# Sparse attention's keys and queries laid out by half heads: an elementwise rotary step and logits of two 64-row products

## The chip, the cores and the metric

The program runs on one core of one Trainium2 chip. The metric is the device time of one execution in microseconds (us), the median of several. Before the change it is 1267.69 us (three runs, 1267.61 to 1268.04).

## The reference, cut to what matters

One first block (16 meta tokens and 256 tokens of width 1024, a gated delta rule branch, a sparse attention branch, an MLP) is followed by a second block. The change touches the sparse attention branch alone. Its queries have 8 heads of 128, its keys 2 heads of 128 (query head h goes with key head h // 4), and both are rotated by position:

```python
def _apply_rope(x, cos, sin):
    half = x.shape[-1] // 2
    xf = x.astype(jnp.float32)
    x1, x2 = xf[..., :half], xf[..., half:]
    ...
    return jnp.concatenate([x1 * c - x2 * s, x2 * c + x1 * s], axis=-1).astype(x.dtype)

def _dsa_branch(q, k, v, qi, ki, wi, rope_att, rope_idx, n_visible):
    q = _apply_rope(q.reshape(B_, T_, ATT_HEADS, ATT_HD), cos_a, sin_a)
    k = _apply_rope(k.reshape(B_, T_, ATT_KV_HEADS, ATT_HD), cos_a, sin_a)
    qi = _apply_rope(qi.reshape(B_, T_, IDX_HEADS, IDX_HD), cos_i, sin_i)
    ki = _apply_rope(ki.reshape(B_, T_, 1, IDX_HD), cos_i, sin_i)[:, :, 0]
    ...
        s = jnp.einsum('bqhd,bsd->bqhs', qib, ki)
        s = jnp.einsum('bqhs,bqh->bqs', jax.nn.relu(s), wib).astype(jnp.float32)
        ...
        _, idx = lax.top_k(s, topk)
        ...
        logits = jnp.einsum('bqgrd,bqkgd->bqgrk', qg, k_sel).astype(jnp.float32) * (ATT_HD ** -0.5)
```

## The kernel before, in words

**Weights.** All projections read one stream of 1 MB slots (`stream`, 256 output columns each). SyncE fetches slot s + 4 into the ring of four when TensorE has finished slot s (`slot_done`). ScalarE rounds a slot to fp32r (`whi`, line 506), VectorE, or for six slots GpSimd, makes the rest (`wlo`, lines 513 and 831), and TensorE adds three products for every tile (line 540, `mm3`), 48 matmuls for a slot. So nearly all of TensorE's time is line 540 and, for the layers that end on tokens, line 702.

**The attention part.** TensorE, ScalarE and VectorE all walk the list `PROJECT`, each doing its part of a step. The slots are `iq` (2), `av`, `ak`, `aq` (4), then `gb`, `z` and `ga` (4 each, the gates). A projection lands in one of two double banks of PSUM, and ScalarE copies it out (`project_out`, lines 1059 to 1070) and frees the pair (`pair_free`). A `rot` step is the rotary step of one tile or two: TensorE multiplies them by a signed permutation (`rotation`, line 2391, constant `turna` or `turni`) into one of the four small PSUM banks (`aux`), and VectorE makes ctmp = turned x sin (line 1655), x = x cos (line 1658), x = x + ctmp (line 1659) in `rotate`. Steps 0 to 2 are the index key and the index queries, 3 and 4 the two key heads, 5 to 8 the query heads two by two. The query rotations lag: the queries of slot j are turned after slot j + 1, the last ones after two eighths of gate slot 0.

**Selection.** `("idx", t, half)` makes four index heads' scores for query block t: TensorE (line 2400) multiplies 64-row operands, even heads in partitions 0 to 63, odd ones in 64 to 127. ScalarE takes relu, VectorE sums them (lines 1672 and 1675). `("top", t)` finds the 64 largest of each row on VectorE in eight rounds (lines 1688 and 1689), and leaves a bias (lines 1690 and 1692). The width is 144 for t = 0 and 272 for t = 1.

**Logits.** When `rope` stands at 9 (all nine rotations are done), TensorE makes one 128-row matmul a head (line 2431) into an `aux` bank; VectorE scales it and adds the bias (line 1762), takes the maximum (line 1766); ScalarE takes exponentials. The logits stand between pieces of gate slots: `gate_part(n, k0, k1)` does the eighths k0 to k1 of slot n, six matmuls each.

```python
            gate_part(0, 0, 2)
            rotation(8)
            gate_part(0, 2, 5)
            pe.wait_ge(S("rope"), 9)
            logits(0, 0, 4)
            ...
            for q in range(4):
                logits(1, 2 * q, 2 * q + 2)
                gate_part(1, q, q + 1)
```

GpSimd makes the rest of gate slot 0 once `rope` is 6, of slots 1 and 2 once it is 9.

Of the kernel before, what the change touches and what calls it, by code (L numbers as in the profile page):

```python
# [21 lines left out]
ALU = mybir.AluOpType  # L22
# [3 lines left out]
P = 128  # L26
D = 1024
KT = D // P
NCOL = 256
META = 16  # L30
QLO = META - 4
SEQ = 256
# [32 lines left out]
for _name, _count in PARAMS:  # L65
# [5 lines left out]
CONST1 = [("ident", 128), ("window", 32), ("upper", 128), ("upper16", 128), ("ones16", 128), ("spread", 128), ("head", 8),  # L71
          ("levels", 4 * 128), ("cosa", T1), ("sina", T1), ("cosi", T1), ("sini", T1), ("turna", 128),
          ("turni", 128), ("past", 2 * T1)]
# [8 lines left out]
for _name, _count in CONST2:  # L82
# [7 lines left out]
PROJECT = [("rot", 0), ("iq", 0), ("iq", 1), ("rot", 1), ("rot", 2), ("av", 0), ("idx", 0, 0), ("lo", "aq", 1), ("l2", 0),  # L90
           ("l2t", 0), ("sel", 0), ("idx", 0, 1), ("ak", 0), ("avt", 0), ("top", 0), ("cum", 0), ("idx", 1, 0), ("lo", "aq", 2), ("rot", 3), ("rot", 4),
           ("aq", 0), ("idx", 1, 1), ("lo", "aq", 3), ("aq", 1), ("rot", 5), ("top", 1), ("aq", 2), ("rot", 6), ("aq", 3),
           ("rot", 7)]

# [47 lines left out]
def program(nc, stream, params, const1, const2, x_in, x_tok, gains, y_out):  # L142
    ctx = ExitStack()
    with ctx:
# [249 lines left out]

        ROT = ["rot_ik", "rot_iq0", "rot_iq1", "rot_ak0", "rot_ak1"] + [f"rot_aq{n}" for n in range(4)]
        for step in PROJECT:
# [6 lines left out]
            elif step[0] in ("l2", "l2t", "sel", "cum"):  # L403
                use_next({"l2": "l2sum"}.get(step[0], step[0]))
        use_next(ROT[8])
        for t in range(2):
            use_next(*[f"log{t}_{hh}" for hh in range(H1)])
        for t in range(2):
# [430 lines left out]
        def pool_body(pool, own):  # L839

            pool.wait_ge(S("rope"), 6)
            pool_low(pool, FIRST["gb"], FIRST["gb"] + 1)
            pool.wait_ge(S("rope"), 9)
            pool_low(pool, FIRST["gb"] + 1, FIRST["gb"] + 3)
            pool.wait_ge(S("prob"), 4)
            pool_low(pool, FIRST["z"], FIRST["z"] + 3)

            pool.wait_ge(S("nglo"), 4)
            pool.dma_start(c2[:], const2).then_inc(c2_in, 16)
            pool.dma_start(ht[:], x_tok).then_inc(S("ht_in"), 16)  # L850
            pool.wait_ge(S("merged"), 4)
            pool_gain(pool, "wout")
            pool.wait_ge(S("h_postmix"), 9)
            pool_gain(pool, "down")

            pool.wait_ge(S("rqk"), 1)
            pool_gain(pool, "ro")
            for k in range(2):
                def tail(s0, it, j):

                    n0 = k * FT2 + j
                    pool.wait_ge(S("f_silu"), n0 + 1 + 4 * it)
                    if n0 >= 2:
                        pool.wait_ge(S("f_hi"), n0 - 1 + 4 * it)
                    nc.gpsimd.tensor_tensor(fu[:, s0 % 2], fs[:, s0 % 2], ft[:, s0 % 2, 1], ALU.mult)\  # L865
                        .then_inc(S("f_prod"), 1)
                    pool.wait_ge(S("f_prod"), n0 + 1 + 4 * it)
                    pool.wait_ge(S("f_hi"), n0 + 1 + 4 * it)
                    nc.gpsimd.tensor_tensor(flo[:, bass.ds(j + 4 * it, 1)], fu[:, s0 % 2].unsqueeze(1),
                                            fhi[:, bass.ds(j + 4 * it, 1)].bitcast(F32), ALU.subtract).then_inc(S("f_lo"), 1)  # L870
                slots(pool, f"fu{k}", tail)
                pool.wait_ge(S(["h_postret", "h_postdiff"][k]), 9)
                pool_gain(pool, f"fd{k}")
                if k == 0:
                    pool.wait_ge(S("dn_root"), 1)
                    pool_gain(pool, "do")
# [744 lines left out]
        def dve_body(dve, own):  # L1621
# [29 lines left out]
            def rotate(step):  # L1651
# [8 lines left out]
                dve.wait_ge(S("rope"), step + 1)  # L1660

            def scores(t, half):

# [75 lines left out]
            for step in PROJECT:  # L1739
                if step[0] == "iq":  # L1740
                    load_lo(FIRST["iq"] + step[1] + 3, 0)
                elif step[0] == "rot":
                    rotate(step[1])
                    if step[1] == 2:
                        decay_finish()
                elif step[0] == "idx":
                    scores(step[1], step[2])
# [6 lines left out]
                elif step[0] == "lo":  # L1754
                    low_of(step[1], step[2])
            rotate(8)
            for t in range(2):
                W = META + P + t * P
                lm = lms[t]
                for hh in range(H1):  # L1760
# [3 lines left out]
                for hh in range(4, 8):  # L1764
                    after(dve, f"log{t}_{hh}")
# [329 lines left out]
        def rotations():  # L2095
            yield "rot_ik", ik[:].unsqueeze(1), T1, "cosi", "sini", 0
            for n in range(2):
                yield f"rot_iq{n}", iq[:, 2 * n:2 * n + 2], SEQ, "cosi", "sini", META
            for n in range(2):
                yield f"rot_ak{n}", ak[:, n:n + 1], T1, "cosa", "sina", 0  # L2100
            for n in range(4):
                yield f"rot_aq{n}", aq[:, 2 * n:2 * n + 2], SEQ, "cosa", "sina", META

# [222 lines left out]
        def pe_body(pe):  # L2326
# [51 lines left out]
            def rotation(step):  # L2378
                name, x, W, c, sn, t0 = todo[step]
                turn = cst("turni" if c == "cosi" else "turna")  # L2380
                if name == "rot_ik":
                    pair_done(pe, 0)
                elif name[:6] == "rot_iq":
                    pair_done(pe, pair_first["iq"] + int(name[6:]))
                elif name[:6] == "rot_ak":
                    pair_done(pe, pair_first["ak"])
                else:
                    pair_done(pe, pair_first["aq"] + int(name[6:]))
                b = fill(name)
# [37 lines left out]
            def logits(t, h0, h1):  # L2427
                W = META + P + t * P
                for hh in range(h0, h1):
                    b = fill(f"log{t}_{hh}")  # L2430
                    is_full(nc.tensor.matmul(b[:, 0:W], aq[:, hh, t * P:t * P + P], ak[:, hh // 4, 0:W], start=True,
                                             stop=True), f"log{t}_{hh}")

            for step in PROJECT:
# [14 lines left out]
                elif step[0] in STEP_SLOTS:  # L2449
                    project(step[0], step[1])  # L2450
            gate_part(0, 0, 2)
            rotation(8)
            gate_part(0, 2, 5)
            pe.wait_ge(S("rope"), 9)
            logits(0, 0, 4)
# [545 lines left out]
def constants():  # L3001
# [14 lines left out]
    for tag, dim in (("a", 128), ("i", 64)):  # L3016
        inv = (f(10000.0) ** (-np.arange(0, dim, 2, dtype=f) / f(dim))).astype(f)
        ang = pos[None, :] * inv[i % (dim // 2)][:, None]
        c["cos" + tag], c["sin" + tag] = np.cos(ang), np.sin(ang)
        turn = np.zeros((P, P), f)  # L3020
        for m in range(P):
            lo = m % dim < dim // 2
            turn[m + dim // 2 if lo else m - dim // 2, m] = -1.0 if lo else 1.0
        c["turn" + tag] = turn
    past = [np.where(pos[None, :] <= (META + t * P + i)[:, None], 0.0, -BIG) for t in range(2)]
# [13 lines left out]
def laid_out(v):  # L3039
    w = v["w_in"][0]  # L3040
    at = np.cumsum([0, 1024, 1024, 1024, 1024, 8, 8, 1024, 256, 256, 512, 64, 8, 1024, 1024])
    gq, gk, gv, gz, gb, ga, aq, ak, av, iq, ik, iw, gate_a, gate_b = (w[:, a:b] for a, b in zip(at[:-1], at[1:]))
    small = np.concatenate([ik, ik, gb, ga, iw, np.zeros((D, NCOL - 152), w.dtype)], 1)
    ain = v["a_w_in_2"][0]
    kv = v["w_kv_2"]
# [55 lines left out]
```

## Time and profile before

| what | value |
|---|---|
| median of three runs | 1267.69 us (1267.61, 1267.69, 1268.04) |
| span of the profiled execution, first to last instruction | 1268.2 us |
| TensorE matmuls | 9041, busy 1254.3 us (99%) |
| TensorE weight loads | busy 1169.6 us (92%) |
| VectorE | busy 919.6 us (73%) |
| ScalarE | busy 699.2 us (55%) |
| GpSimd | busy 154.3 us (12%) |
| DMA queue of the weights | 46.9% of 16 engines' span |
| mean granted clock of TensorE | 0.998 of full speed |

The span stands 0.5 us above the median; no time of its own but the span is recorded for the profiled execution. In the profile PE is TensorE's matmuls, PEld its weight loads, DVE VectorE, ACT ScalarE, POOL GpSimd. Matmuls overlap in the array, so the durations of single ones add up to more than the time they take; what one costs is read from start to start. A matmul of plain fp32 operands has two records and two weight loads for each instruction, one of fp32r operands has one. The attention part lies between 90 and 210 us of the span.

### The profile page before, as it was taken

How to read it: one execution, taken by the hardware profiler on the slowest of the kernel's cores; microseconds unless marked ns; L12 is line 12 of the kernel's file. 1: busy time of each engine (PE TensorE's matmuls, PEld its weight loads, DVE VectorE, ACT ScalarE, POOL GpSimd, SP SyncE). 2: the span in 40 equal slices, each digit the busy share in tenths (PEclk: the TensorE clock that was granted, in tenths of full speed). 3: DMA queues.
4: the chain of work that ended last, by engine and by line, in shares of the span. 5: the costliest groups of instructions: out<-in, count | busy, mean ns of one | idle time of the engine just before them, and what ended most of it. 6: DMA issues, size and time to landing. Idle time of an engine off the chain costs nothing.

```text
span 1268.2 us, 23324 instructions
## 1 busy us (share of the span) xinstructions
PE 1254.3 (99%) x9041; PEld 1169.6 (92%) x9041; DVE 919.6 (73%) x1290; ACT 699.2 (55%) x1082; POOL 154.3 (12%) x113
## 2 busy tenths in 40 slices
PE   9999999999999999999999999999999999999998
PEld 8997999999989998889998989999889998999986
DVE  6886874878778774447734547999758777999954
ACT  5556465654456343345354546666547567766642
POOL 0000142000000000000000001642200000464310
PEclk9999999999999999999999999999999999999999
DMA  7552332322355555555553444555564444454562
GB/s 300 189 173 101 133 134 101 133 68 68 152 197 188 195 179 185 198 170 182 183 209 109 156 173 167 198 169 195 194 221 171 162 154 163 167 188 175 197 224 93
DMA packets 30315, 212.83 MB, mean 168 GB/s; under 512 B 3488, under 2 KB 3616, under 8 KB 5152
## 3 DMA queue, kind: packets, MB, share of 16 engines
q1 hardware_dynamic: 29088, 206.53, 46.9%
q0 software_dynamic: 1152, 5.24, 1.1%
q8 instruction: 55, 0.90, 0.3%
q14 instruction: 20, 0.16, 0.0%
HBM read 210.71 MB, written 1.05 MB: 167 GB/s over the span
## 4 chain that ended last, share of the span: by engine, by line
PE 86%; DVE 8%; ACT 4%; DMA 1%; issue 1%; SPq 0%; DVEq 0%; ACTq 0%
PE lin L540 50%; PE lin L702 21%; DVE wlo L513 3%; PE lin L2883 2%; PE lin L567 2%; ACT whi L506 2%; PE lin L569 1%; DMA raw<-in_stream 1%; PE aux L2627 1%; PE aux L2599 1%; PE aux L2485 1%; ACT lm L1377 1%; PE aux L725 1%; PE aux L2745 1%; PE aux L2555 1%
## 5 line engine op out<-in xcount | busy, mean ns | idle before, releaser
L513 DVE TENSOR_TENSOR wlo<-raw,whi 128x2048 fp32r<-128x2048 f32 x183 | 427.4, 2338 | 170.8 <-ACT whi L506 170.1
L506 ACT CAST whi<-raw 128x2048 fp32r<-128x2048 f32 x192 | 365.3, 1906 | 179.5 <-DMA raw<-in_stream 147.0
L540 PE MATMUL lin<-xhi,whi 128*128 128x256 f32 (+2 forms) x1616 | 461.5, 286 | 1.0 <-DVE wlo L513 1.0
L540 PE MATMUL lin<-xlo,whi 128*128 128x256 f32 (+2 forms) x1616 | 457.0, 283 | 0.0
L540 PE MATMUL lin<-xhi,wlo 128*128 128x256 f32 (+2 forms) x1616 | 454.7, 281 | 0.0
L540 PEld LDWEIGHTS lin<-xhi,whi 128*128 128x128 f32 x1616 | 304.1, 188 | 3.0 <-DVE wlo L513 1.2
L540 PEld LDWEIGHTS lin<-xhi,wlo 128*128 128x128 f32 x1616 | 306.1, 189 | 0.0
L540 PEld LDWEIGHTS lin<-xlo,whi 128*128 128x128 f32 x1616 | 304.6, 189 | 0.4
L865 POOL TENSOR_TENSOR fu<-fs,ft 128x256 f32<-128x256 f32 x44 | 86.2, 1958 | 259.4 <-ACT fs L1479 259.4
L2292 DVE SCALAR_TENSOR_TENSOR ft<-fy,par,ft 128x254 f32<-128x254 f32 (+1 forms) x176 | 109.5, 661 | 5.9 <-DVE ft L2292 0.2
L540 PE MATMUL lin<-whi,xhi 128*128 128x256 f32 x256 | 74.2, 290 | 0.0
L540 PE MATMUL lin<-wlo,xhi 128*128 128x256 f32 x256 | 71.9, 281 | 0.0
L540 PE MATMUL lin<-whi,xlo 128*128 128x256 f32 x256 | 71.8, 280 | 0.0
L702 PE MATMUL lin<-whi,flo 128*128 128x512 f32 x176 | 70.2, 399 | 0.0
L702 PE MATMUL lin<-wlo,fhi 128*128 128x512 f32 x176 | 69.4, 394 | 0.0
L702 PE MATMUL lin<-whi,fhi 128*128 128x512 f32 x176 | 69.1, 393 | 0.0
L1479 ACT ACTIVATE fs<-ft 128x256 f32<-128x256 f32 x44 | 18.4, 419 | 70.1 <-DVE ft L2292 70.1
L1471 ACT ACTIVATE ft<-fy,par 128x256 f32<-128x256 f32 x88 | 48.2, 595 | 15.4 <-DVE fy L2284 15.4
L837 POOL DMA_DIRECT2D gp<-in_gains x6 | 3.3, 549 | 409.0 <-DVE top L2124 241.8
L702 PE MATMUL lin<-whi,ulo 128*128 128x512 f32 x128 | 51.1, 399 | 0.0
L702 PE MATMUL lin<-wlo,uhi 128*128 128x512 f32 x128 | 50.4, 394 | 0.0
L702 PE MATMUL lin<-whi,uhi 128*128 128x512 f32 x128 | 50.3, 393 | 0.0
(454 smaller groups left out, 2123.2 us busy)
## 6 DMA issues: line engine op xcount, KB each, us to landing
raw<-in_stream SPq DMA_DIRECT2D x193, 1024.0 KB, 4.9
gp<-in_gains POOLq DMA_DIRECT2D x6, 512.0 KB, 3.9
c<-in_const SPq DMA_DIRECT2D x1, 1460.0 KB, 16.0
h<-in_x SPq DMA_DIRECT2D x2, 544.0 KB, 4.4
c<-in_const POOLq DMA_DIRECT2D x1, 1024.0 KB, 6.5
ht<-in_xtok POOLq DMA_DIRECT2D x1, 1024.0 KB, 9.6
out<-ht SPq DMA_DIRECT2D x1, 512.0 KB, 2.6
out<-ht SPq DMA_DIRECT2D x2, 256.0 KB, 2.0
```

The costliest lines, as they stand in the source:

```text
L506: nc.scalar.copy(whi[:, s0 % 4], raw[:, s0 % 4]).then_inc(hi_ready, 1)
L513: nc.vector.tensor_tensor(wlo[:, s0 % 4], raw[:, s0 % 4], whi[:, s0 % 4].bitcast(F32), ALU.subtract).then_inc(lo_ready, 1)
L540: ins = nc.tensor.matmul(out, a, b, start=start and n == 0, stop=stop and n == 2)
L567: nc.tensor.matmul(out, hi[:, kt, a], w[:, s0 % 4, kt], start=kt == 0 and n == 0, stop=False)
L569: ins = nc.tensor.matmul(out, lo[:, kt, a], whi[:, s0 % 4, kt], start=False, stop=kt == KT - 1)
L702: ins = nc.tensor.matmul(PS[u % 2][:, c], a, b[:, kt - first], start=g == 0 and kt == first and n == 0, stop=g == group - 1 and kt == end ...
L725: ins = nc.tensor.transpose(AUX[bank][:, at + c * P:at + c * P + P], ht[:, c, kt * P:kt * P + P], ident)
L865: nc.gpsimd.tensor_tensor(fu[:, s0 % 2], fs[:, s0 % 2], ft[:, s0 % 2, 1], ALU.mult)\
L1471: ins = nc.scalar.activation(ft[:, p, t], fy[:, p, t], ACT.Identity, scale=pdyn(f"f_conv{k}", (t * FT2 + j) * 3 + 2 + 12 * it), bias=pdyn( ...
L1479: nc.scalar.activation(fs[:, p], ft[:, p, 0], ACT.Silu).then_inc(S("f_silu"), 1)
L2292: ins = nc.vector.scalar_tensor_tensor(ft[:, p, t, sh:SEQ], fy[:, p, t, 0:SEQ - sh], pdyn(f"f_conv{k}", col), ft[:, p, t, sh:SEQ], ALU.mul ...
L2883: ins = nc.tensor.matmul(PS[u % 2][:, c], a, b[:, kt - 4 * g], start=kt == 0 and n == 0, stop=kt == KT - 1 and n == 2)
```

## The change

The columns of the key and query weights are laid out anew on the host (`laid_out`): of the keys, tile 0 holds the first halves of both heads, head 0 in partitions 0 to 63 and head 1 in 64 to 127, and tile 1 the second halves; of the queries, slot j's two tiles hold the first and the second halves of heads j and j + 4 in the same way. The two halves that the rotary step mixes now stand in the same partitions of two tiles. So:

- the permutation products for keys and queries (rotations 3 to 8) and the constant `turna` go; those of the index part stay;
- VectorE's step `rope(n)` makes ctmp0 = x sin and ctmp1 = x cos for both tiles at once, then tile 0 = ctmp1[0] - ctmp0[1] and tile 1 = ctmp1[1] + ctmp0[0], four instructions for the keys (before: six in two steps) and four for each query slot (before: three). It waits for ScalarE's copy alone;
- in `PROJECT`, `("rope", 0)` takes the place of the two key rotations, `("rope", 1..3)` the places of the query rotations, and `rope(4)` the place of the last; in TensorE's order nothing stands there any more. The waits on `rope` are lower by one;
- the logits of heads j and j + 4 are made together, each as two 64-row matmuls that accumulate in its bank, in turn on partitions 0 to 63 and 64 to 127. Twice as many matmul instructions, of half the rows.

```diff
-           ("l2t", 0), ("sel", 0), ("idx", 0, 1), ("ak", 0), ("avt", 0), ("top", 0), ("cum", 0), ("idx", 1, 0), ("lo", "aq", 2), ("rot", 3), ("rot", 4),
-           ("aq", 0), ("idx", 1, 1), ("lo", "aq", 3), ("aq", 1), ("rot", 5), ("top", 1), ("aq", 2), ("rot", 6), ("aq", 3),
-           ("rot", 7)]
+           ("l2t", 0), ("sel", 0), ("idx", 0, 1), ("ak", 0), ("avt", 0), ("top", 0), ("cum", 0), ("idx", 1, 0), ("lo", "aq", 2), ("rope", 0),
+           ("aq", 0), ("idx", 1, 1), ("lo", "aq", 3), ("aq", 1), ("rope", 1), ("top", 1), ("aq", 2), ("rope", 2), ("aq", 3),
+           ("rope", 3)]
+HEADS = (0, 4, 1, 5, 2, 6, 3, 7)
...
-            pool.wait_ge(S("rope"), 6)
+            pool.wait_ge(S("rope"), 5)
...
-            pool.wait_ge(S("rope"), 9)
+            pool.wait_ge(S("rope"), 8)
...
+            def rope(n):
+                j = n - 1
+                x, c, s = ((aq[:, 2 * j:2 * j + 2], cst("cosa", lo=META, n=SEQ), cst("sina", lo=META, n=SEQ)) if n else
+                           (ak[:], cst("cosa"), cst("sina")))
+                W = x.shape[2]
+                pair_done(dve, pair_first["aq"] + j if n else pair_first["ak"])
+                nc.vector.tensor_tensor(ctmp[:, 0, :, 0:W], x, bc(s, 2), ALU.mult)
+                own.link(nc.vector.tensor_tensor(ctmp[:, 1, :, 0:W], x, bc(c, 2), ALU.mult))
+                nc.vector.tensor_tensor(x[:, 0], ctmp[:, 1, 0, 0:W], ctmp[:, 0, 1, 0:W], ALU.subtract)
+                nc.vector.tensor_tensor(x[:, 1], ctmp[:, 1, 1, 0:W], ctmp[:, 0, 0, 0:W], ALU.add).then_inc(S("rope"), 1)
+                dve.wait_ge(S("rope"), 4 + n)
...
             def logits(t, h0, h1):
                 W = META + P + t * P
-                for hh in range(h0, h1):
-                    b = fill(f"log{t}_{hh}")
-                    is_full(nc.tensor.matmul(b[:, 0:W], aq[:, hh, t * P:t * P + P], ak[:, hh // 4, 0:W], start=True,
-                                             stop=True), f"log{t}_{hh}")
+                for pair in range(h0, h1, 2):
+                    names = [f"log{t}_{hh}" for hh in HEADS[pair:pair + 2]]
+                    banks = [fill(name) for name in names]
+                    for half in range(2):
+                        for g in range(2):
+                            r = slice(64 * g, 64 * g + 64)
+                            ins = nc.tensor.matmul(banks[g][:, 0:W], aq[r, pair + half, t * P:t * P + P], ak[r, half, 0:W],
+                                                   start=half == 0, stop=half == 1)
+                            if half:
+                                is_full(ins, names[g])
...
-            gate_part(0, 0, 2)
-            rotation(8)
-            gate_part(0, 2, 5)
-            pe.wait_ge(S("rope"), 9)
+            gate_part(0, 0, 5)
+            pe.wait_ge(S("rope"), 8)
             logits(0, 0, 4)
...
+    ak = ak.reshape(D, 2, 2, 64).transpose(0, 2, 1, 3).reshape(D, NCOL)
+    aq = aq.reshape(D, 2, 4, 2, 64).transpose(0, 2, 3, 1, 4).reshape(D, 1024)
```

**TensorE, the first logits.** Before: the last matmul of the gate slot's first five eighths, the logits of heads 0 to 3 for t = 0, and the gate slot going on (`aux` are the small banks, `aq` and `ak` queries and keys, `lin` the double banks).

```order
L540 MATMUL lin1<-xhi_81,wlo_50 128x256
L2431 MATMUL aux3<-ak_85,aq_84 128x144 [waits aux_free3,rope]
L2431 MATMUL aux0<-ak_85,aq_84 128x144 [waits aux_free0]
L2431 MATMUL aux1<-ak_85,aq_84 128x144 [waits aux_free1]
L2431 MATMUL aux2<-ak_85,aq_84 128x144 [waits aux_free2]
L540 MATMUL lin1<-xhi_81,whi_51 128x256
```

And with the change, the same place:

```order
L540 MATMUL lin1<-xhi_81,wlo_50 128x256
L2439 MATMUL aux1<-ak_85,aq_84 128x144 [waits aux_free2,aux_free1,rope]
L2439 MATMUL aux2<-ak_85,aq_84 128x144
L2439 MATMUL aux1<-ak_85,aq_84 128x144
L2439 MATMUL aux2<-ak_85,aq_84 128x144
L2439 MATMUL aux3<-ak_85,aq_84 128x144 [waits aux_free0,aux_free3]
L2439 MATMUL aux0<-ak_85,aq_84 128x144
L2439 MATMUL aux3<-ak_85,aq_84 128x144
L2439 MATMUL aux0<-ak_85,aq_84 128x144
L540 MATMUL lin1<-xhi_81,whi_51 128x256
```

The four heads' matmuls have become eight, two by two on the same pair of banks, and the wait on `rope` stands at the same point of the gate slot.

**VectorE, from the end of the second selection to the first logits.** Before (`ibias_b` is the bias of t = 1, `c_77` the constants):

```order
L1692 SCALAR_TENSOR_TENSOR ibias_b<-ibias_b,c_77 128x272 [waits dve_own]
L1655 TENSOR_TENSOR ctmp<-aux,c_77 128x2x256 [waits aux_full0,dve_own]
L1658 TENSOR_TENSOR aq<-aq,c_77 128x512 [waits aux_free0]
L1659 TENSOR_TENSOR aq<-aq,ctmp 128x512 [waits dve_own]
L1655 TENSOR_TENSOR ctmp<-aux,c_77 128x2x256 [waits aux_full1,rope]
L1658 TENSOR_TENSOR aq<-aq,c_77 128x512 [waits aux_free1]
L1659 TENSOR_TENSOR aq<-aq,ctmp 128x512 [waits dve_own]
L1655 TENSOR_TENSOR ctmp<-aux,c_77 128x2x256 [waits aux_full2,rope]
L1658 TENSOR_TENSOR aq<-aq,c_77 128x512 [waits aux_free2]
L1659 TENSOR_TENSOR aq<-aq,ctmp 128x512 [waits dve_own]
L1762 SCALAR_TENSOR_TENSOR lm<-aux,ibias 128x144 [waits aux_full3,rope]
```

With the change, the same place up to the last `rope` step's last instruction:

```order
L1669 TENSOR_TENSOR ctmp<-aq,c_77 128x2x256 [waits pair_free0,dve_own]
L1670 TENSOR_TENSOR ctmp<-aq,c_77 128x2x256
L1671 TENSOR_TENSOR aq<-ctmp 128x256 [waits dve_own]
L1672 TENSOR_TENSOR aq<-ctmp 128x256
L1669 TENSOR_TENSOR ctmp<-aq,c_77 128x2x256 [waits pair_free1,rope]
L1670 TENSOR_TENSOR ctmp<-aq,c_77 128x2x256
L1671 TENSOR_TENSOR aq<-ctmp 128x256 [waits dve_own]
L1672 TENSOR_TENSOR aq<-ctmp 128x256
L1669 TENSOR_TENSOR ctmp<-aq,c_77 128x2x256 [waits pair_free0,rope]
L1670 TENSOR_TENSOR ctmp<-aq,c_77 128x2x256
L1671 TENSOR_TENSOR aq<-ctmp 128x256 [waits dve_own]
L1672 TENSOR_TENSOR aq<-ctmp 128x256
```

Three instructions on two tiles have become two on two tiles and two on one tile each; the wait on TensorE's bank (`aux_full`) has become one on ScalarE's copy (`pair_free`).

## Rows read from the trace of the kernel before

**Rows 1.** Busy time by engine, and shares of the chain that ended last (the page).
```profile
PE 1254.3 (99%) x9041; PEld 1169.6 (92%) x9041; DVE 919.6 (73%) x1290; ACT 699.2 (55%) x1082; POOL 154.3 (12%) x113
PE 86%; DVE 8%; ACT 4%; DMA 1%; issue 1%; SPq 0%; DVEq 0%; ACTq 0%
```

**Rows 2.** The chain of waits from 88 to 335 us: start us, us, what.
```profile
146.89 0.70 DVE ctmp L1655
...
163.99 0.70 DVE aq L1659
164.74 1.25 PE aux L2431 x8
...
174.87 9.22 PE lin L540 x78
```

**Rows 3.** Timeline at the rotations: start us, us, engine, line, what (matrix, moving), times.
```profile
132.15 1.19 PE L2391 MATMUL aux<-ak,c 128*128 128x272 f32 x4
...
133.29 0.28 PE L540 MATMUL lin<-xlo,whi 128*128 128x256 f32 x1
...
158.81 0.28 PE L540 MATMUL lin<-xhi,wlo 128*128 128x256 f32 x1
158.92 1.02 PE L2391 MATMUL aux<-aq,c 128*128 128x256 f32 x4
...
159.91 0.28 PE L540 MATMUL lin<-xlo,whi 128*128 128x256 f32 x1
```

**Rows 4.** Timeline where the first logits wait, and a pair of heads of t = 1.
```profile
164.10 0.28 PE L540 MATMUL lin<-xhi,wlo 128*128 128x256 f32 x1
164.74 1.25 PE L2431 MATMUL aux<-ak,aq 128*128 128x144 f32 x8 [0.36 <-DVE aq L1659]
164.76 4.56 POOL L831 TENSOR_TENSOR wlo<-raw,whi 128x2048 fp32r<-128x2048 f32 x1 [11.03 <-DVE aq L1659]
...
168.80 0.28 PE L540 MATMUL lin<-xhi,wlo 128*128 128x256 f32 x1
168.92 1.08 PE L2431 MATMUL aux<-ak,aq 128*128 128x272 f32 x4
...
170.07 0.28 PE L540 MATMUL lin<-xhi,wlo 128*128 128x256 f32 x1
```

**Rows 5.** TensorE's timeline at the 64-row index scores of t = 1, four heads.
```profile
138.72 0.28 PE L540 MATMUL lin<-xhi,wlo 128*128 128x256 f32 x1
138.93 1.19 PE L2400 MATMUL aux<-ik,iq 64*128 64x272 f32 x8
...
140.26 0.28 PE L540 MATMUL lin<-xlo,whi 128*128 128x256 f32 x1
140.38 0.29 PE L540 MATMUL lin<-xhi,wlo 128*128 128x256 f32 x1
```

**Rows 6.** VectorE's timeline before the logits, and a 128x256 operation near the end.
```profile
141.81 2.32 DVE L1675 SCALAR_TENSOR_TENSOR iscore<-irelu,wix,iscore 128x272 f32<-128x272 f32 x4 [1.75 <-ACT irelu L1079]
144.04 2.29 DVE L513 TENSOR_TENSOR wlo<-raw,whi 128x2048 fp32r<-128x2048 f32 x1
146.89 0.69 DVE L1655 TENSOR_TENSOR ctmp<-aux,c 128x512 f32<-128x512 f32 x1 [0.56 <-PE aux L2391]
147.62 0.69 DVE L1658 TENSOR_TENSOR aq<-aq,c 128x512 f32<-128x512 f32 x1
...
1262.95 0.42 DVE L1524 TENSOR_TENSOR yt<-lin,gp 128x256 f32<-128x256 f32 x1 [3.00 <-ACT junk L963]
```

**Rows 7.** Stretches: window, us, busy us (x) by engine, PEclk, DMA share, GB/s.
```profile
109.50:112.90 3.40, 2.05 (x16) 1.09 (x16) 2.81 (x10) 1.89 (x6) 0.00 (x0) 1.00 0.51 147
119.07:122.48 3.41, 2.76 (x23) 2.31 (x23) 1.72 (x10) 1.53 (x6) 0.00 (x0) 1.00 0.00 0
122.48:125.89 3.41, 3.41 (x17) 3.41 (x16) 2.96 (x13) 1.18 (x2) 0.00 (x0) 0.50 0.01 2
125.89:129.30 3.41, 3.41 (x29) 3.41 (x28) 2.65 (x12) 0.00 (x0) 0.00 (x0) 1.00 0.00 0
```

More of the change, by code:

```diff
@@ L71 @@
 CONST1 = [("ident", 128), ("window", 32), ("upper", 128), ("upper16", 128), ("ones16", 128), ("spread", 128), ("head", 8),
-          ("levels", 4 * 128), ("cosa", T1), ("sina", T1), ("cosi", T1), ("sini", T1), ("turna", 128),
+          ("levels", 4 * 128), ("cosa", T1), ("sina", T1), ("cosi", T1), ("sini", T1),
           ("turni", 128), ("past", 2 * T1)]
@@ L393, in use_next @@
                 turn_at[0] += 1
-        ROT = ["rot_ik", "rot_iq0", "rot_iq1", "rot_ak0", "rot_ak1"] + [f"rot_aq{n}" for n in range(4)]
+        ROT = ["rot_ik", "rot_iq0", "rot_iq1"]
         for step in PROJECT:
@@ L404, in program @@
                 use_next({"l2": "l2sum"}.get(step[0], step[0]))
-        use_next(ROT[8])
         for t in range(2):
-            use_next(*[f"log{t}_{hh}" for hh in range(H1)])
+            use_next(*[f"log{t}_{hh}" for hh in HEADS])
         for t in range(2):
@@ L1745, in dve_body @@
                         decay_finish()
+                elif step[0] == "rope":
+                    rope(step[1])
                 elif step[0] == "idx":
@@ L1755, in dve_body @@
                     low_of(step[1], step[2])
-            rotate(8)
+            rope(4)
             for t in range(2):
@@ L1759, in dve_body @@
                 lm = lms[t]
-                for hh in range(H1):
+                for hh in HEADS:
                     b = full(dve, f"log{t}_{hh}")
@@ L1763, in dve_body @@
                                                            ALU.mult, ALU.add), f"log{t}_{hh}")
-                for hh in range(4, 8):
+                for hh in HEADS[4:]:
                     after(dve, f"log{t}_{hh}")
@@ L2098, in rotations @@
                 yield f"rot_iq{n}", iq[:, 2 * n:2 * n + 2], SEQ, "cosi", "sini", META
[L2099 to L2102, printed above, removed]
         def dve_second(dve, own):
@@ L2379, in rotation @@
                 name, x, W, c, sn, t0 = todo[step]
[L2380 to L2388, printed above, removed]
+                turn = cst("turni")
+                pair_done(pe, 0 if name == "rot_ik" else pair_first["iq"] + int(name[6:]))
                 b = fill(name)
@@ L3019, in constants @@
         c["cos" + tag], c["sin" + tag] = np.cos(ang), np.sin(ang)
[L3020 to L3024, printed above, removed]
+    turn = np.zeros((P, P), f)
+    for m in range(P):
+        lo = m % 64 < 32
+        turn[m + 32 if lo else m - 32, m] = -1.0 if lo else 1.0
+    c["turni"] = turn
     past = [np.where(pos[None, :] <= (META + t * P + i)[:, None], 0.0, -BIG) for t in range(2)]
```

## The prediction

> **What bounds the kernel now.** The page comes first: TensorE's matmuls fill 99% of the span, and the chain that ended last is TensorE's for 86% and VectorE's for 8% [rows 1]. That would say that TensorE's time is the price of everything. But the share is an average, so the second view is the chain of waits over the attention part. There one piece is not TensorE's: from 146.89 us, where VectorE takes up the first query rotation, to the end of its last one at 164.69, the chain is VectorE's without a break (a rotation, the second selection with its eight rounds, three rotations); then come the logits and TensorE's gate slots [rows 2]. Third, the timeline at the end of that piece: TensorE's last gate matmul starts at 164.10, the logits at 164.74 instead of 0.12 later, so it waits 0.5 us for VectorE [rows 4]. In this stretch the two engines are nearly level. What TensorE is spared before 164 is worth something only as far as VectorE is early too; what it is given after 164.7 costs in full, because from there on it does not stop. Last come the rows for prices: rotations, logits, and the index scores, which are 64-row matmuls already [rows 3 to 5].
>
> **What TensorE loses before the wait.** A query rotation is two instructions, four records of 256 columns. Line 540 goes on at 158.81, 159.60, 159.91; between the first and the last of these 1.10 us pass where two steps of 0.12 would, so it costs 0.86 us [rows 3]. Four of them are 3.44. The two key rotations are four records of 272 columns, like the logits of two heads of t = 1: from 168.80 to 170.07 are 1.27 us, less three steps of 0.12, so 0.91 [rows 4]; their own rows, 132.15 to 133.29, say the same [rows 3]. Together TensorE would stand at the wait 4.35 us earlier, its last matmul starting at 159.75.
>
> **When VectorE gets there.** Three things move its end at 164.69.
> - The key rotations stand before the second half of the second scores. Those come 0.91 earlier, and with them ScalarE's relu, for which VectorE waits 1.75 us [rows 6]. VectorE's own part before it, the key step, gets shorter and stays hidden in that wait. Gain 0.91.
> - After the rest of a weight slot (start 144.04, 2.29 long) VectorE waits 0.56 us for the turned queries; the new step needs only ScalarE's copy of queries that were finished 7 us before. The row before shows that an instruction that waits for nothing starts 0.09 before the end of its predecessor (141.81 + 2.32 against 144.04) [rows 6]. Gain 0.65.
> - The step itself: three dependent instructions of 128x512, one every 0.73 us (146.89, 147.62), are 2.18. The new one is two of 512 elements, of which the second doesn't wait (0.60 + 0.73), and two of 256, 0.42 long in the nearest row, of which the second doesn't wait either (0.33 + 0.46): 2.12 [rows 6]. Four times, gain 0.24. No gain if the reads across two tiles are slower, and 0.5 at most if they overlap more.
>
> So `rope` is full 1.8 us earlier, and the logits start at 162.9. Of TensorE's 4.35 us only 1.8 arrive; the wait grows from 0.5 us to 3.1, some 2.9 of them without any matmul running.
>
> **What TensorE gains after the wait.** Twice as many instructions of half the rows. Do two halves run side by side? The index scores answer: eight records of 64 rows and 272 columns last 1.19 us, four records of 128 rows and the same columns 1.08 [rows 4, 5]. They overlap two by two, in the order in which the new logits come as well (partitions 0 to 63, then 64 to 127). A pair of heads is now eight such records, as those four index heads are. Line 540 around them: 138.72 to 140.38, 1.66 us less three steps of 0.12, so 1.30 [rows 5], where the pair costs 0.91 now. The 0.4 more are not columns; they lie before the group, after its first records and behind it, once for every group of 64-row matmuls between 128-row ones. The Trainium skill (TensorEngine Tiling, Key Properties) says that changing the tiling mode, not the tile, drains the engine; by this rule too a group pays once however many matmuls it has, and the rows above can't say otherwise. There are seven groups: three for t = 0, four for t = 1. Six at 0.4, and the first 0.3, because it starts from idle anyway: 2.7 us. Bounds: 0 (the switch is hidden where line 540's weights are loaded ahead) and 3.5 (0.5 each, if accumulating into one bank delays the second half).
>
> **The other engines.** VectorE's reads of the logits follow pair by pair, and TensorE's next pair of the same two banks comes two groups later, as before. GpSimd makes the rest of gate slot 1 from the last `rope` on, 4.56 us from 164.76 [rows 4]; TensorE needs it after the first logits of t = 1, at 169.64 before, 4.9 us after the wait; now 1.6 us more lie between, so it is on time. The constants' DMA is 65 KB smaller, at the start, behind the first projections: nothing. ScalarE does the same work.
>
> **The sum so far.** -1.8 + 2.7 = +0.9 us. TensorE's chain goes on without a stop behind it [rows 2], so this stays.
>
> **And the clock.** In one stretch of the whole span TensorE was granted half its clock (the lower of its two levels, 1.2 of 2.4 GHz): 122.48 to 125.89. Just before it, from 119.07, it had 2.76 us of short matmuls and gaps in 3.41; in the half-clock stretch only 17 matmuls ran where the next stretch has 29 [rows 7]. Twelve fewer at 0.12 to 0.125 are 1.5 us. Elsewhere a stretch with 2.05 us busy of 3.40 kept the full clock [rows 7]. A hole of 2.9 us without a matmul is deeper than either. I take it that it lowers the clock more often than not, and that part of the half-clock stretch falls into the wait itself: +1.1 to +1.7, I take 1.4. The Trainium skill (TensorE: Matmul & The Clock Gate, Why this matters for your kernels) warns that an idle gap between bursts brings the lower level back; no row here has such a long gap in mid-kernel, and by that rule the clock falls here. Sum: +2.3 us.
>
> The sum is made against the profiled execution, whose span of 1268.2 stands 0.5 above the median; I add it to the median: 1267.7 + 2.3 = **1270.0 us**. A measurement of this kernel tells 0.2%, 2.5 us, from no change, so "no change" is from 1265.2 to 1270.2.
>
> **Rivals.**
> - *The clock holds.* For it: the stretch that was busy for less than the one before the fall and kept it, so busy time alone doesn't decide [rows 7]. Then +0.9: 1268.6 us. Chance 0.29.
> - *The halves don't overlap* (the other side, slower). For it: the new matmuls accumulate in two banks, the index scores went to four. Eight heads of t = 1 then cost 0.46 more each (half of 0.91), eight of t = 0 about 0.24 (columns 144 of 272): 5.6 us more, with the switches +6.5, 1274.2. It decides from 0.1 us a head on, since +0.9 and 16 x 0.1 reach the 2.5. Against it: the order of rows is that of the index scores, which overlap. Chance 0.07.
> - *The switch costs nothing, or a later wait takes the delay.* Then the 1.8 us of the earlier `rope` stay in part: 1265.9 to 1267.6. For it: line 540's weight loads may hide it; against it: the rows show 0.4 even so. Chance 0.14, of which 0.05 for a gain of over 0.2%, which needs VectorE's steps shorter as well.
> - *`rope` is full no earlier than before* (ScalarE's copies or relus turn out late, and VectorE waits for them). Then the 1.8 us are gone and the 2.7 stay: 1270.4 us, and with a lower clock up to 1271.8. Against it: the copies are finished 7 us ahead of the steps that read them, but for the last. Chance 0.06.
>
> The forecast itself, +0.9 and a lower clock, has 0.44; its own range is 1269.4 to 1270.7. A range for 8 in 10 takes in the case without the clock and the nearer part of the third: 1266.5 to 1271.2. Slower by over 0.2%: 0.14 of the forecast's upper part, 0.07, and the last case, 0.26. Faster: 0.05. The rest, 0.69, is no change.
>
> **What would show it.** In the profile after: no record of the permutation for keys and queries; VectorE without an idle time before the first query step and its last `rope` at about 162.9; TensorE idle for some 2.9 us in front of the first logits, the largest hole of the kernel; sixteen heads' logits as 64 records, eight of them in about 1.2 us for t = 1 and in 0.8 for t = 0; a stretch of half clock that begins within 2 us of the hole's end. I am wrong if the hole is under 2 us (VectorE's end moves with TensorE after all), if eight records take 2 us (no overlap), if the steps from line 540 into the logits and out again are no longer than before, or if the clock stays at 1.

## The result, and the profile after

| | before | changed |
|---|---|---|
| median of 9 runs | 1267.94 us | 1271.66 us |
| lowest to highest | 1267.32 to 1268.14 | 1268.84 to 1274.17 |
| the profiled execution: time, span | some 1270.0 (an estimate: 1268.2 + 1.8), 1268.2 | 1270.51, 1268.6 |
| mean granted clock over the runs | | 1.0 in the lowest run, 0.996 to 0.998 in the others |

The changed kernel takes 1.0026 times as long, 95% interval 1.0018 to 1.0034: 3.7 us more. The forecast was 1270.0, with a range to 1271.2; the median lies 0.5 us above the range. The second row says more than the first: before scatters over 0.8 us in these nine runs (over 2.1 in 28 later ones), the change over 5.3, and its one run at a full clock, 1268.84, stands 0.9 above the median of before. That is the prediction's sum without its clock term.

A remark on reading: the profiled run of the change took 1270.51 us and has a span of 1268.6; time less span is 1.75 to 1.86 us in the later runs of before and 1.86 to 2.05 in those of the change and its variants. The prediction compared the span of before (1268.2) with the median of the times. That execution took some 1270.0, above the common time of its kernel: of 28 later runs of before, 24 lie between 1267.42 and 1268.45 and four at 1269.22 to 1269.54. Its half-clock stretch at 122 us [rows 7] seems to be what such executions pay for. Two of the experiments' profiles below have it too, e2_rope_warm's and e6_one's, and these executions lie 1.4 and 1.5 us above the medians of their kernels. The profiles of e1_warm, e1_warm6 and e3_halves_only, all within 0.4 us of their medians, don't have it, nor do the seven profiles of kernels with a hole of 3 us or more in front of the logits.

The page after, busy times and shares of the chain that ended last (it answers to [rows 1]):

```profile
PE 1251.1 (99%) x9053; PEld 1165.1 (92%) x9053; DVE 918.5 (72%) x1292; ACT 699.4 (55%) x1082; POOL 154.7 (12%) x113
PE 87%; DVE 8%; ACT 4%; issue 1%; DMA 1%; DVEq 0%; SPq 0%; ACTq 0%
```

TensorE is busy for 3.2 us less and the kernel is no faster: the page alone shows neither the hole nor the clock. The timeline of TensorE after, at the first logits and at the first pair of t = 1 (start us, us, engine, line, what; the idle time before in brackets):

```profile
157.88 0.28 PE L540 MATMUL lin<-xhi,wlo 128*128 128x256 f32 x1
161.14 2.29 PE L2439 MATMUL aux<-ak,aq 64*128 64x144 f32 x16 [2.98 <-DVE aq L1672]
163.36 0.58 PE L540 MATMUL lin<-xhi,whi 128*128 128x256 f32 x1
...
167.78 0.28 PE L540 MATMUL lin<-xhi,wlo 128*128 128x256 f32 x1
167.99 1.19 PE L2439 MATMUL aux<-ak,aq 64*128 64x272 f32 x8
...
169.45 0.28 PE L540 MATMUL lin<-xhi,wlo 128*128 128x256 f32 x1
...
174.05 1.19 PE L2439 MATMUL aux<-ak,aq 64*128 64x272 f32 x8
```

The last gate matmul before the wait starts at 157.88, the logits only at 161.14; TensorE is idle for 2.98 us in front of them, where it was 0.36 [rows 4]. (All stands some 1.8 us earlier here than in the trace of before, because the stretch at 122 us kept its clock.) The 16 records of the first group take 2.29 us, where the same 16 take 1.25 at full clock (an experiment below). The pair of t = 1 costs 169.45 - 167.78 - 3 x 0.12 = 1.31 us, as the index scores had said [rows 5]. The stretches of the same place (window, us, busy us (x) of PE, PEld, DVE, ACT, POOL, PEclk, DMA share, GB/s):

```profile
157.73:161.14 3.41, 0.43 (x5) 0.23 (x3) 3.25 (x7) 1.04 (x4) 0.00 (x0) 1.00 0.34 142
161.14:164.55 3.41, 3.41 (x21) 3.13 (x22) 1.04 (x4) 0.00 (x0) 3.39 (x1) 0.50 0.02 5
164.55:167.97 3.42, 3.42 (x31) 2.75 (x29) 1.18 (x5) 0.00 (x0) 3.34 (x2) 1.00 0.00 0
```

The stretch behind the hole is granted 0.50, the lower of the two levels; in this execution the next one is whole again. And VectorE's steps after (timeline):

```profile
141.33 2.29 DVE L513 TENSOR_TENSOR wlo<-raw,whi 128x2048 fp32r<-128x2048 f32 x1
143.54 0.69 DVE L1669 TENSOR_TENSOR ctmp<-aq,c 128x512 f32<-128x512 f32 x1
144.14 0.69 DVE L1670 TENSOR_TENSOR ctmp<-aq,c 128x512 f32<-128x512 f32 x1
144.86 0.43 DVE L1671 TENSOR_TENSOR aq<-ctmp 128x256 f32<-128x256 f32 x1
145.20 0.42 DVE L1672 TENSOR_TENSOR aq<-ctmp 128x256 f32<-128x256 f32 x1
145.65 0.45 DVE L1701 MAX8 top<-iscore 128x8 f32<-128x272 f32 x1
...
160.66 0.42 DVE L1672 TENSOR_TENSOR aq<-ctmp 128x256 f32<-128x256 f32 x1
```

Nothing is waited for between the weight slot and the first query step, and a step takes 143.54 to 145.65, 2.11 us. From the start of the weight slot to the end of the last step are 161.08 - 141.33 = 19.75 us, before 164.69 - 144.04 = 20.65: 0.9 less, the prediction's 0.65 and 0.24. The other 0.91 lies before the weight slot.

### The profile page after: what moved, and what is told of

It is laid out like the page before. It is cut to its first block, busy times and chain, and to the rows that moved or that the text cites. A ratio compares the mean times of both kernels' runs of the same rounds, so it can differ in the third digit from the quotient of the medians.

```text
span 1268.6 us, 23350 instructions
## 1 busy us (share of the span) xinstructions
PE 1251.1 (99%) x9053; PEld 1165.1 (92%) x9053; DVE 918.5 (72%) x1292; ACT 699.4 (55%) x1082; POOL 154.7 (12%) x113
## 4 chain that ended last, share of the span: by engine, by line
PE 87%; DVE 8%; ACT 4%; issue 1%; DMA 1%; DVEq 0%; SPq 0%; ACTq 0%
PE lin L540 50%; PE lin L702 22%; DVE wlo L513 3%; PE lin L567 2%; PE lin L2891 2%; ACT whi L506 2%; PE lin L569 1%; PE aux L2635 1%; PE aux L2607 1%; PE aux L725 1%; PE aux L2493 1%; PE aux L2439 1%; ACT lm L1377 1%; PE aux L2753 1%; PE aux L2563 1%
## 6 DMA issues: line engine op xcount, KB each, us to landing
ht<-in_xtok POOLq DMA_DIRECT2D x1, 1024.0 KB, 10.2
```

## The experiments

**Theories.** A: the sum without the clock (+0.9) is right, and the hole costs the rest, since the chip grants half the clock behind it, in some runs for longer than in the profile above. B: the 64-row matmuls cost more than the trace shows, or themselves pull the clock down, hole or no hole. C: half of each (a hole with 128-row logits costs one stretch, and the 64-row ones make it longer).

The first four ran beside 28 runs of before (median 1267.76).

**e0_again**, the changed kernel once more.

> The changed kernel once more, for the spread of its times and a second profile. Theory A (the clock): the times scatter by some 2 to 5 us from a floor near 1268.8, the floor being the run at full clock (before + 0.9), and each excess goes with a mean granted clock under 1, by one or more half-clock stretches after the hole of 3 us in front of the first logits. Theory B (the 64-row matmuls or something else of the change is slow by itself in some executions): the scatter doesn't go with the granted clock.

Measured: 1271.56 us (7 runs, 1268.69 to 1272.15), ratio 1.0024 [1.0012, 1.0035]. The one run at clock 1.0 took 1268.69. This time the profiled execution is of the median kind (the stretches from the logits on, same columns):

```profile
158.71:162.12 3.41, 0.98 (x16) 0.98 (x16) 2.43 (x6) 0.07 (x1) 0.95 (x1) 1.00 0.04 17
162.12:165.54 3.42, 3.42 (x21) 2.65 (x18) 1.07 (x5) 0.00 (x0) 3.42 (x1) 0.50 0.02 5
165.54:168.95 3.41, 3.41 (x18) 2.91 (x19) 0.96 (x5) 0.00 (x0) 3.33 (x2) 0.50 0.00 0
168.95:172.36 3.41, 3.41 (x26) 2.47 (x25) 2.08 (x3) 2.08 (x11) 1.36 (x1) 1.00 0.49 125
```

Two stretches at half clock, with TensorE without a stop in both. This run is 2.9 us over the one at full clock; the run profiled first, with one such stretch, was 1.7 over. For the price by the traces, here are the weight slot before the query steps and the last group of logits:

```profile
141.34 2.28 DVE L513 TENSOR_TENSOR wlo<-raw,whi 128x2048 fp32r<-128x2048 f32 x1
175.48 1.19 PE L2439 MATMUL aux<-ak,aq 64*128 64x272 f32 x8
```

From the one to the other are 34.14 us here and 174.05 - 141.33 = 32.72 in the first profile.

**e1_warm** fills the hole with matmuls that have no use (the bank is overwritten by the first logits).

```
+            b = fill("log0_0")
+            for _ in range(12):
+                nc.tensor.matmul(b[:, 0:P], ones[:], ones[:], start=True, stop=True)
             pe.wait_ge(S("rope"), 8)
```

> The changed kernel with twelve dummy products of 128x128 ones into the still empty first logit bank, issued before the wait on rope, some 2.7 us of TensorE work in a hole of 3 us. Nothing real moves. Theory A (the hole lowers the clock): the scatter goes, the time is before + 0.9, 1268.7 to 1269.1, no half-clock stretch after 160 us. Theory B (the scatter comes from the 64-row logits, or from elsewhere): still 1270 to 1272 with a spread of 4 us.

Measured: 1269.05 us (11 runs, 1268.59 to 1270.58), 1.0010 [1.0001, 1.0019]. The weight slot, TensorE's timeline and the stretches there:

```profile
141.97 2.28 DVE L513 TENSOR_TENSOR wlo<-raw,whi 128x2048 fp32r<-128x2048 f32 x1
158.64 2.84 PE L2464 MATMUL aux<-ones 128*128 128x128 f32 x24
161.76 1.25 PE L2439 MATMUL aux<-ak,aq 64*128 64x144 f32 x16 [0.28 <-DVE aq L1672]
173.11 1.19 PE L2439 MATMUL aux<-ak,aq 64*128 64x272 f32 x8
```

```profile
158.60:162.00 3.40, 3.12 (x30) 2.93 (x30) 3.00 (x7) 0.81 (x4) 0.22 (x1) 1.00 0.28 113
162.00:165.40 3.40, 3.40 (x36) 2.88 (x34) 1.47 (x6) 0.00 (x0) 3.40 (x1) 1.00 0.00 0
```

The same logits, at the same moment after the weight slot (19.79 us here, 19.81 with the hole), behind matmuls instead of a hole: the clock stays at 1.00, the first group takes 1.25 us instead of 2.29, and 2.5 us are back. From the weight slot to the last logits are 31.14 us, so one stretch at half clock cost 32.72 - 31.14 = 1.6 us and two cost 34.14 - 31.14 = 3.0. What is left is the sum without the clock (+0.9 expected, +1.3 measured).

**e3_halves_only**: the kernel before, with the 64-row logits and the new order of heads alone.

> The kernel before, its permutation products and its layout kept, with the logits alone as pairs of 64-row matmuls in the new order of heads (leaves out the right pairing of the halves). My sum: seven groups, six at 0.4 us and one at 0.3 to 0.4, so before + 2.7 to 2.8, 1270.7, with little scatter, since TensorE waits there for 0.5 us only. Theory B: scatter of several us here too, without a hole. If the halves did not overlap: before + 8.

Measured: 1270.45 us (10 runs, 1270.18 to 1272.02), 1.0024 [1.0014, 1.0033]: +2.7, the seven groups' price to the tenth. The wait is 0.33 us there and no stretch near the logits loses its clock. So 64-row matmuls alone do not pull it down, which is against the second half of B.

**e2_rope_warm**: the elementwise step, the filled hole, and one 128-row matmul a head.

> The changed kernel with the dummies and with one 128-row matmul a head for the logits, as before (leaves out the right pairing of the halves: the logits are of other sums). It is the elementwise rotary step alone. My sum gives the logits 1.8 us earlier and nothing behind it: before - 1.8, 1266.1. If a tiling switch costs nothing (the rival), it equals the run with 64-row logits and dummies. If the delay were absorbed later, it would stand at before - 0.5 or higher.

Measured: 1266.37 us (11 runs, 1265.96 to 1267.78), 0.9988 [0.9979, 0.9997]: -1.4, where -1.8 was expected. In the traces the whole 1.8 are there (the weight slot before the key step and the first logits; of before, whose logits start at 164.74 [rows 4], the weight slot first):

```profile
135.04 2.28 DVE L513 TENSOR_TENSOR wlo<-raw,whi 128x2048 fp32r<-128x2048 f32 x1
...
134.91 2.28 DVE L513 TENSOR_TENSOR wlo<-raw,whi 128x2048 fp32r<-128x2048 f32 x1
162.81 1.25 PE L2435 MATMUL aux<-ak,aq 128*128 128x144 f32 x8 [0.29 <-DVE aq L1672]
```

That is 29.70 us before and 27.90 here. Where the 0.4 us between trace and median goes is not shown. The earlier `rope` is real, and it is the 64-row logits that give it back: e1_warm, the same with them, is 2.7 us longer, the price of the seven groups once more.

The next four ran beside 21 runs of before (median 1267.87).

**e2_rope_only**: the same without the filling.

> The elementwise rotary step with 128-row logits (leaves out the right pairing of the halves) and no dummies: the hole of 3 us is there, the 64-row logits are not. Theory A (the hole lowers the clock): floor 1266.1 to 1266.4 as with the dummies, but most runs 1 to 4 us above it, median 1267.5 to 1269. Theory B (the 64-row logits are needed for the scatter): as with the dummies, 1266.4, spread 1 us.

Measured: 1267.88 us (11 runs, 1265.86 to 1269.97), 1.0001 [0.9992, 1.0010]. Its lowest run (1265.86) has the time of the filled version's lowest (1265.96); the median lies 1.5 above the filled version's. The stretches behind the hole:

```profile
162.43:165.84 3.41, 3.41 (x17) 3.41 (x17) 1.25 (x5) 0.00 (x0) 3.41 (x1) 0.50 0.00 0
165.84:169.25 3.41, 3.41 (x24) 3.18 (x24) 2.60 (x5) 0.75 (x4) 3.33 (x2) 1.00 0.26 34
```

One stretch, near the 1.4 of the prediction: 8 of the 11 runs lie 1.7 to 2.3 over the lowest, two 3.6 and 4.1 over it. The changed kernel, with 64-row logits, lies 2.8 or more over the lowest run of its series in 9 of 16 runs (e0_again's among them). That speaks for C, but counts so small can differ by chance. And a time alone does not tell two stretches behind the hole (3.0 us) from one there and the one at 122 us: kernels without the hole lie some 1.5 to 2 us over the rest in about one run of seven, so the two runs here may be of that kind. The nine cannot all be, and e0_again's profile shows two in a row.

**e1_warm6** halves the filling (6 for 12).

> The changed kernel with six dummies in place of twelve, so that a hole of about 1.6 us is left. Theory A, by degrees: a hole of 1.5 us kept the clock at 109.6 us in the kernel before, so mostly 1268.8 to 1269.1 and now and then one half-clock stretch of 1.5 us. If the lower clock came from the wait as such and not from its length, 1270 to 1272.

Measured: 1268.91 us (11 runs, 1268.51 to 1270.67), 1.0010 [1.0001, 1.0019], as with twelve. The gap in front of the logits is 1.65 us, and the profile has no half-clock stretch there; behind one of 2.98 it was lost in 8 runs of 9, by their times and mean clocks. (The gap at 109.9 us in the kernel before, which the expectation puts at 1.5 us, is one of 1.2.) The few runs of both filled versions at 1270.4 to 1270.7 lie as far out as the few of before at 1269.2 to 1269.7.

**e4_fill** and **e5_two** fill the hole with work that must be done anyway: all of gate slot 0 and an eighth of slot 1. So that slot 1 is there in time, GpSimd's wait on the last `rope` goes. e4 has the logits in four groups, e5 in two. The edit of e5 (e4's differs in where the logits stand):

```
-            gate_part(0, 0, 5)
+            gate_part(0, 0, 8)
+            gate_part(1, 0, 1)
             pe.wait_ge(S("rope"), 8)
...
+            logits(0, 0, 8)
+            gate_part(1, 1, 3)
+            logits(1, 0, 8)
+            gate_part(1, 3, 4)
...
-            pool.wait_ge(S("rope"), 8)
             pool_low(pool, FIRST["gb"] + 1, FIRST["gb"] + 3)
```

> The changed kernel with real work in the hole: all of gate slot 0 and an eighth of slot 1 before the wait on rope (2.8 us), GpSimd's rest of slots 1 and 2 no longer held back by rope, and the logits in four groups of four heads in place of seven groups. TensorE: 4.35 us of products gone, the wait of before (0.5) gone, four groups at 0.4 us: before - 3.2, 1264.5, no half-clock stretch after 160 us. If groups are not what a switch is paid for, but matmuls, before - 2.1. If GpSimd beside VectorE's selection slows it, the logits start later than 161.2.

> The same with two groups of eight heads, so two switches in place of four: 0.8 us less, but for t = 0 VectorE must read four banks faster than TensorE fills them (0.52 us a pair against 0.46), a stall of 0.2 to 0.5: before - 3.6, 1264.1. If the stall takes more, VectorE's reads are the bound of a group: 1264.5 to 1265.

Measured: 1273.85 us (5 runs), 1.0049 [1.0035, 1.0062], and 1273.18 (5 runs), 1.0043 [1.0029, 1.0057]. The hoped-for gain is a loss of 6.0 and 5.3 us. The timeline of VectorE and of GpSimd in e4 tells why:

```profile
154.02 2.66 DVE L1702 SCALAR_TENSOR_TENSOR ibias_b<-iscore,eps 128x272 f32<-128x272 f32 x1
156.71 0.44 DVE L1704 SCALAR_TENSOR_TENSOR ibias_b<-ibias_b,c 128x272 f32<-128x272 f32 x1
157.19 0.69 DVE L1668 TENSOR_TENSOR ctmp<-aq,c 128x512 f32<-128x512 f32 x1
157.80 5.08 DVE L1669 TENSOR_TENSOR ctmp<-aq,c 128x512 f32<-128x512 f32 x1
```

```profile
151.75 4.62 POOL L831 TENSOR_TENSOR wlo<-raw,whi 128x2048 fp32r<-128x2048 f32 x1 [1.02 <-ACT whi L506]
157.42 4.91 POOL L831 TENSOR_TENSOR wlo<-raw,whi 128x2048 fp32r<-128x2048 f32 x1 [1.05 <-ACT whi L506]
```

A VectorE product of 0.69 us takes 5.08: it ends 0.5 us after GpSimd's subtraction, which began 0.4 us before it, is done (162.33). The logits start only at 167.98, and TensorE idles 6.8 us in front of them, more than the hole that was to be filled. Behind so long a hole the half clock lasts longer too; it begins in the hole:

```profile
163.61:173.85 10.24, 5.87 (x38) 5.25 (x38) 5.75 (x15) 0.00 (x0) 0.00 (x0) 0.50 0.11 46
```

Three more ran beside another 21 runs of before (median 1268.12).

**e7_pool_early** tests that by itself: the changed kernel with the filling of e1, and only GpSimd's wait taken away.

> The changed kernel with the twelve dummies, and only GpSimd's wait on the last rope dropped, to tell what made the kernels with real work in the hole slow. If GpSimd's subtraction blocks VectorE's two-operand instructions (one of 512 elements lasted 5.08 us beside it), the logits start 6 to 7 us later than with the dummies alone: 1269 + 6 and one or more half-clock stretches, 1275 to 1278. If the order of the gate slots was the cause, 1269.

Measured: 1278.94 us (5 runs, 1276.94 to 1279.46), 1.0085 [1.0071, 1.0099]. The forecast ended at 1278, 0.9 us lower. The logits start 26.35 us after the weight slot, e1_warm's 19.79: 6.6 us of the 9.5 over e1_warm (each against its own runs of before). For the rest, TensorE has half the clock from 163.49 to 173.73, 5.9 us of it after the logits' start, where half the time is 2.9. It is 4.8 us longer than e4, which does 2.8 us of gate matmuls in the hole and has three groups fewer (1.2 us). VectorE's timeline:

```profile
152.96 0.45 DVE L1700 MAX8 top<-iscore 128x8 f32<-128x272 f32 x1
...
153.98 2.65 DVE L1702 SCALAR_TENSOR_TENSOR ibias_b<-iscore,eps 128x272 f32<-128x272 f32 x1
...
157.75 5.01 DVE L1669 TENSOR_TENSOR ctmp<-aq,c 128x512 f32<-128x512 f32 x1
```

**e6_one** leaves GpSimd's wait as it is, and fills the hole with the three eighths that are there: gate slot 0 whole before the wait, then all logits of both tiles in one group.

```
-            gate_part(0, 0, 5)
+            gate_part(0, 0, 8)
             pe.wait_ge(S("rope"), 8)
...
+            logits(0, 0, 8)
+            logits(1, 0, 8)
+            gate_part(1, 0, 4)
             gate_part(1, 4, 8)
```

> The changed kernel with GpSimd held back as it was, the rest of gate slot 0 (three eighths, 2.1 us) before the wait on rope, and all the logits of t = 0 and t = 1 in one group, then gate slot 1. The hole shrinks to 0.9 us, one tiling switch in place of seven; against it stalls for VectorE's reads, 0.6 to 1.2 us together. Logits start at before - 1.8, one switch 0.3, stalls 0.9, gate work of 2.1 less behind: before - 2.7, 1265.1, no half-clock stretch after 160 us, no scatter. If the stalls make a hole of their own or a long stretch of 64-row matmuls lowers the clock: 1266.5 to 1268.

Measured: **1266.05 us** (11 runs, 1265.73 to 1267.77), 0.9985 [0.9976, 0.9994]: 2.1 us below the kernel before and 5.6 below the change, faster than both, though by less than 0.2%. TensorE's timeline:

```profile
162.68 1.25 PE L2439 MATMUL aux<-ak,aq 64*128 64x144 f32 x16 [0.86 <-DVE aq L1672]
164.21 1.25 PE L2439 MATMUL aux<-ak,aq 64*128 64x144 f32 x16 [0.28 <-DVE lm L1777]
165.65 2.10 PE L2439 MATMUL aux<-ak,aq 64*128 64x272 f32 x16 [0.18 <-DVE lm L1777]
168.32 2.10 PE L2439 MATMUL aux<-ak,aq 64*128 64x272 f32 x16 [0.57 <-DVE lm_b L1777]
```

The hole is down to 0.86 us and the clock stays there. (The profiled execution took 1267.51 us, 1.5 over the median, and has the stretch at 122 us:)

```profile
122.16:125.57 3.41, 3.41 (x17) 3.41 (x16) 2.98 (x12) 1.27 (x2) 0.00 (x0) 0.50 0.01 2
```

Six of the seven groups' prices are gone; in their place TensorE waits 0.28, 0.18 and 0.57 us for VectorE to read the banks, 1.0 us where 0.9 were expected. That is a small part of the 0.6 us by which it missed -2.7; the rest is not explained.

**e8_t1_whole**: the changed kernel, hole and all, with one 128-row matmul a head for t = 1 alone.

```
+                if t:
+                    for hh in HEADS[h0:h1]:
+                        b = fill(f"log{t}_{hh}")
+                        is_full(nc.tensor.matmul(b[:, 0:W], aq[:, hh, t * P:t * P + P], ak[:, hh // 4, 0:W], start=True,
+                                                 stop=True), f"log{t}_{hh}")
+                    return
```

> The changed kernel, hole included, with 64-row matmuls for the logits of t = 0 alone and one 128-row matmul a head for t = 1 (leaves out the right pairing there). Four switches fewer: floor 1268.8 - 1.6 = 1267.2. If the 64-row matmuls after the hole hold the clock down for a second stretch, the median excess over the floor is that of whole-row logits (1.5 us: 1268.7); if the t = 0 group alone suffices for it, it is that of the changed kernel (2.6 to 2.8 us: 1270).

Measured: 1268.84 us (11 runs, 1267.29 to 1270.70), 1.0010 [1.0001, 1.0019]. The stretches behind its hole:

```profile
161.51:164.92 3.41, 3.41 (x24) 2.91 (x22) 1.04 (x4) 0.00 (x0) 3.41 (x1) 0.50 0.02 5
164.92:168.33 3.41, 3.41 (x30) 2.92 (x31) 1.54 (x5) 0.00 (x0) 3.33 (x2) 1.00 0.00 0
```

The lowest run stands at the expected floor (1267.29 for 1267.2): four groups fewer are worth 1.6 us. The profiled run has one stretch, and the median lies 1.55 over the lowest run. But four of the 11 runs lie 2.8 to 3.4 over it; the longer loss may be there too, or in part the stretch at 122 us. Nor can the form of t = 1 have caused the longer loss in the changed kernel: in e0_again both half-clock stretches are over at 168.95, and its first logits of t = 1 start at 169.40. C, in the form in which this run was to test it, is not borne out; what is left of it is the 64-row logits of t = 0, or chance.

## Why the prediction was wrong

Its steps, one by one:

- *Before the wait TensorE is spared 4.35 us, of which 1.8 arrive.* Right: the hole is 2.98 us where 2.9 were forecast. The last `rope` comes 0.9 earlier from the weight slot on, as worked out, and the version with nothing else in it (e2_rope_warm) has its logits 1.8 earlier in the trace, of which its median shows 1.4.
- *The seven groups cost 2.7 us.* Right: the pair costs 1.31 us for 1.30, and e3 is 2.7 slower. The halves do overlap (1.19 us for eight records of 272 columns), so the rival that they don't has fallen, and so has the one in which the switch costs nothing.
- *The sum +0.9.* Right to 0.4 us: 1268.84 and 1268.69 in the two runs at full clock, each 0.9 above the median of its runs of before, and 1.3 and 1.0 above it with the hole filled (1269.05 and 1268.91).
- *The clock falls behind the hole.* Right: in 8 runs of 9 and 6 of 7, by their times and mean clocks, and in both profiles. The rule of the Trainium skill that the prediction cited (TensorE: Matmul & The Clock Gate) agrees with this trace: 0.50 from 161.14 on. "The clock holds" had 0.29 and is what 1 run in 8 shows.
- *"+1.1 to +1.7, I take 1.4."* **This term failed.** It priced one half-clock stretch, like the one of before at 122 us, and had no upper end beyond one. The runs show 2.8 us in the median (1271.66 - 1268.84; 2.5 against the filled hole of e1_warm) and up to 5.3: one stretch costs 1.6 (the first profile), two in a row cost 3.0 (e0_again), and 9 of 16 runs lie 2.8 or more over full clock. Nor did part of the stretch fall into the wait, as assumed: it begins with the logits in the first profile (161.14) and 1.0 us after their start in e0_again's. With 2.8 for 1.4 the sum is +3.7 and the time 1267.7 + 3.7 = 1271.4, outside the range of 1271.2. The last 0.3 us to the measured 1271.66 are the median of before, 1267.94 beside the change where 1267.69 had been at hand.

- *"Slower by over 0.2%: 0.26."* A slip without effect: its parts, 0.14, 0.07 and 0.06, make 0.27.

The mechanism was the right one, its size was read from the only neighbour at hand. At 122 us the gaps were short, and one half-clock stretch was all that followed; behind a hole of 3 us the lower level is granted for one stretch or for two. That the hole is the cause is shown: without it (e1, e2_rope_warm, e1_warm6, e3, e6) no stretch near the logits is lost in any profile, whatever form the logits have, and with it (the change twice, e2_rope_only, e8) each profile shows one or two. No row of before could give the number of stretches. With "one or two" as bounds, 1.4 to 3, the forecast's own range would have reached 1267.7 + 0.9 + 3 = 1271.6, the measured median to the tenth and no more.

Three things stay open. What decides between one stretch and two is not known: TensorE ran without a stop in both of e0_again's, and whether the 64-row logits of t = 0 lengthen the loss (9 of 16 runs against 2 of 11 with whole logits) stays open, the more so since the stretch at 122 us may stand behind some of either. The kernel with t = 0 whole and t = 1 in halves was not tried. And what the run of 1274.17 did is not known, since no execution of this kernel beyond 1271.56 was profiled; two stretches behind the hole and one at 122 us would make some 1273.4 (an estimate: 1268.84 + 3.0 + 1.6).

## What to carry to other kernels

Time spared in front of a wait is worth only as much as the engine that is waited for gets earlier, and what remains is a hole that can cost the clock: here 4.35 us of products spared brought the logits 1.8 us forward and bought 3 us idle, which cost 2.8 us by the clock. If such a hole opens, put real work into it and collect the 64-row matmuls in one group (here 0.4 us for each group between 128-row ones); that turned +3.7 us into -2.1. See first what else the wait in front of the hole holds back: with GpSimd let go, the same idea lost 5 to 6 us. For a clock term take the number of stretches as unknown and let the range reach to two, or beyond for a longer hole, and look at the scatter of the runs, not only at one profile.

## What was not expected of the hardware

- **GpSimd's subtraction stops VectorE's.** While GpSimd runs its 128x2048 difference of two SBUF operands (4.6 to 4.9 us), a VectorE instruction that reads two from SBUF lasts until just after it is done: 5.08 and 5.01 us instead of 0.69, 2.66 and 2.65 for a 128x272 operation that takes 0.44 in the changed kernel. A MAX8 in the same 4.6 us took its usual 0.45. The Trainium skill (SBUF — State Buffer, SBUF: two separate sides) calls the pair of ports that the two engines share "an exclusive lock, not a bandwidth split", held for a whole instruction; the trace agrees, 5.08 us against 0.69. So the wait for the last `rope` in GpSimd's program, which looks like lost time, is what keeps VectorE's rotations fast; with the hole filled, its removal alone turns +1.3 us against before (e1) into +10.8 (e7), 6.6 of it later logits and about 2.9 half clock.
- **The half clock behind one and the same hole lasts for one stretch or for two**, 3.4 or 6.8 us, in different runs of one program, and TensorE's matmuls never stop in either. Where the hole was 6.7 to 6.8 us, the half clock began inside it and lasted 10.2 us (e4, e7) or 6.8 (e5). Before scatters over 2.1 us in 28 runs, the change over 5.3 in nine; a scatter like that is a reason to profile more than one execution.
- **Useless matmuls in the hole save more than they cost.** Twelve or six of them in the 3 us, and no stretch behind it is at half clock in either profile; the medians, 1269.05 and 1268.91, stand within 0.2 us of the change's run at full clock, 1268.84.
